# Summing gathered expert rows in 64x64 blocks of the TensorE array, two rows at a time, with one PSUM bank fewer for the context's mixer

## What is computed

```python
qry = (x @ w_query).reshape(n, 8, 2, 128)           # 8 heads
s = einsum('nhpd,hpkd->nhpk', qry, sub_keys)        # 128 keys on either side
# top 16 of each side, top 16 of their sums: 16 experts of 16384 per head and token
w = softmax(top_s)
a = gelu(einsum('nd,nhkd->nhk', xb, expert_u[ib]))  # 128 u rows per token
coef = w * a
x = x + g2 * einsum('nhk,nhkd->nd', coef, expert_v[ib])  # 128 v rows per token
```

## Time and profile before

| | |
|---|---|
| time, three runs | 4953.61, 4959.36, 4966.07 us; median 4959.36 |
| span of the profiled execution, first to last instruction | 4933.1 us |
| its own time beside the span | not listed apart; the median run is 26.3 us above this span |
| mean granted TensorE clock | 0.947 |
| busy share: PE, DVE, GpSimd, ACT | 80%, 62%, 57%, 24% |
| moved by DMA | 1585.40 MB, mean 321 GB/s |
| latents' V places, layer 0 | from 1105 to 2686 us |
| latents' V places, layer 1 | from 3468 to 4900 us |

### The profile page before, as it was taken

One profiled execution on the slowest core, in us unless ns is written; L12 is line 12 of the kernel. 1 busy time (PEld: TensorE's weight loads), 2 busy tenths in 40 slices (PEclk: granted clock), 3 DMA queues, 4 the chain that ended last, 5 costly groups with the idle time before them and its releaser, 6 DMA issues.

```text
span 4933.1 us, 40947 instructions
## 1 busy us (share of the span) xinstructions
PE 3932.0 (80%) x11544; PEld 1863.3 (38%) x11544; DVE 3078.9 (62%) x6951; ACT 1199.2 (24%) x2524; POOL 2831.9 (57%) x2642
## 2 busy tenths in 40 slices
PE   5798889889777777788776787999787777777776
PEld 3674444334333333344342454444332222222222
DVE  8637898775556556555655777852557566566653
ACT  2433333211223222232111343231112111111111
POOL 0001556317677677777766444630767777777775
PEclk8798889999999999999999898999999999999999
DMA  8653889758999999999988766962889999999997
GB/s 306 230 180 144 295 312 389 272 199 318 345 365 358 356 379 379 379 400 400 380 327 336 254 230 238 369 242 79 313 333 379 367 384 383 370 398 383 389 392 299
DMA packets 425891, 1585.40 MB, mean 321 GB/s; under 512 B 47680, under 2 KB 55360, under 8 KB 408640
## 3 DMA queue, kind: packets, MB, share of 16 engines
q0 software_dynamic: 376800, 1394.77, 74.8%
q1 hardware_dynamic: 44256, 183.81, 10.0%
q10 hardware_dynamic: 4608, 4.20, 0.3%
HBM read 1577.87 MB, written 4.72 MB: 321 GB/s over the span
## 4 chain that ended last, share of the span: by engine, by line
PE 20%; DMA 18%; issue 5%; POOL 3%; DVE 2%; ACT 1%; DVEq 1%; ACTq 0%; POOLq 0%
PE pair L744 19%; DMA vbuf_lat<-in_expert_v,idx_lat 17%; POOL ubuf_lat L709 2%; POOL vbuf_lat L716 1%; DVE acc L1747 0%; PE pair L880 0%; PE pair L885 0%; DMA ubuf_ctx<-in_expert_u,idx_ctx 0%; DVE ubuf_ctx L1698 0%; DMA ubuf_lat<-in_expert_u,idx_lat 0%; ACT L1128 0%; DVEq L1569 0%; DVE hist_lat L1566 0%; DVEq L1741 0%; ACT on_lat L1128 0%
## 5 line engine op out<-in xcount | busy, mean ns | idle before, releaser
L744 PE MATMUL pair<-vbuf_lat,diag 128*128 128x512 f32 x4096 | 2036.2, 629 | 706.6 <-DMA vbuf_lat<-in_expert_v,idx_lat 674.6
L744 PEld LDWEIGHTS pair<-vbuf_lat,diag 128*128 128x128 f32 x4096 | 731.8, 195 | 1946.4 <-DMA vbuf_lat<-in_expert_v,idx_lat 1042.3
L716 POOL DMA_INDIRECT vbuf_lat<-in_expert_v,idx_lat x1024 | 1133.9, 1107 | 464.8 <-issue 220.1
L1698 DVE CUSTOM_DVE_ANT_0 ubuf_lat<-hT,ubuf_lat 128x1024 f32<-128x1024 f32 x768 | 936.1, 1224 | 702.2 <-DMA ubuf_lat<-in_expert_u,idx_lat 698.1
L709 POOL DMA_INDIRECT ubuf_lat<-in_expert_u,idx_lat x1024 | 1089.9, 1064 | 376.8 <-issue 226.2
L744 PE MATMUL pair<-hT,slot 128*128 128x512 f32 (+1 forms) x2048 | 578.3, 442 | 24.4 <-DVE hT L1428 15.9
L1128 ACT ACTIVATE diag<-cst,coef 128x128 f32<-128x128 f32 x1024 | 326.6, 390 | 1004.4 <-DVE coef L1704 1000.4
L709 POOL DMA_INDIRECT ubuf_ctx<-in_expert_u,idx_ctx x256 | 292.3, 1142 | 482.7 <-DVE araw L1698 307.3
L1698 DVE CUSTOM_DVE_ANT_0 ubuf_lat<-xnat,ubuf_lat 128x1024 f32<-128x1024 f32 x256 | 312.0, 1224 | 250.4 <-DMA ubuf_lat<-in_expert_u,idx_lat 248.3
L744 PEld LDWEIGHTS pair<-hT,slot 128*128 128x128 f32 x2048 | 319.2, 196 | 275.4 <-issue 262.4
L1128 ACT ACT_TABLE_LOAD x318 | 408.0, 1283 | 31.9 <-DVE mT_lat L1592 15.2
(11 more groups left out here) (313 smaller groups left out, 3148.7 us busy)
## 6 DMA issues: line engine op xcount, KB each, us to landing
slot<-in_w_query SPq DMA_DIRECT2D x32, 1024.0 KB, 5.6
modw<-in_w_mod_turned POOLq DMA_DIRECT2D x28, 1024.0 KB, 5.7
slot<-in_w_qk SPq DMA_DIRECT2D x16, 1024.0 KB, 6.8
slot<-in_w_v SPq DMA_DIRECT2D x16, 1024.0 KB, 5.9
slot<-in_w_r SPq DMA_DIRECT2D x16, 1024.0 KB, 7.9
wraw<-in_w_zg SPq DMA_DIRECT2D x32, 512.0 KB, 6.5
wraw<-in_w_zf SPq DMA_DIRECT2D x32, 512.0 KB, 6.5
wraw<-in_w_gla_out SPq DMA_DIRECT2D x32, 512.0 KB, 6.5
```

The source lines that it names most:

```text
L716: pool.indirect_dma_start(peer[s].v[n % ring_v][:, :], None, v_rows, bass.IndirectOffsetOnAxis(ap=index[:, p // PICKS, p % PICKS:p % PICKS ...
L744: return pe.matmul(out, lhsT, rhs, start=first, stop=last)
L1698: v.tensor_tensor_reduce(rows_of, x, rows_of, 1.0, 0.0, ALU.mult, ALU.add, araw[n % 3][:, p % GS:p % GS + 1]).then_inc(s_dot, 1)
```

## The change

- The latents' V rows are added two places at a time. PE waits for both places' rows and then, for each half of the 1024 columns, issues four matmuls of 64x64 by 64x512: each place's diagonal is cut in its two 64x64 diagonal blocks, which stand in the four different quadrants of the array. The blocks of partitions 0 to 63 write to `pair[0]`, those of 64 to 127 to `pair[1]`; an odd place writes to the other half of the partitions. Both places are marked as added (`s_pv`) by matmuls of the second half of the columns.
- So the sums lie in four banks, in two parts each. ACT makes two copies of 128x1024 at a tile's end, and `turn_latents_out` adds the parts while it transposes: two matmuls by a 128x64 matrix `fold` for each 128 columns, in place of one transpose, now in `ps[7]`.
- `fold` is made by DVE at the start, from the identity; DVE waits for the constants' DMA (`s_const`) ahead of it.
- The context's mixer has `ps[4]` to `ps[6]`. Its products go round three banks; its two state steps share one pair of banks, so the second waits for DVE's update of the first.
- The latents' queries use `ps[6]`, `ps[7]`; the turned natural tiles use `pair[2]` for `pair[0]` (latents) and for `pair[3]` (context, layer 1), with waits that go with this. The first query no longer waits for the context's update; the first V group does.
- `iota` is stored in 32 columns and not 128.

```diff
-                    for j in range(GS):
-                        p = n * GS + j
-                        r = ring_no(l, s, p)
-                        pe.wait_ge(s_gv[s][r % V_RING[s]], gathered(V_RING[s], r))
+                    for j0 in range(0, GS, 2):
+                        for j in (j0, j0 + 1):
+                            r = ring_no(l, s, n * GS + j)
+                            pe.wait_ge(s_gv[s][r % V_RING[s]], gathered(V_RING[s], r))
                         for q in range(2):
-                            last = mm(pair[1][:, q * 512:(q + 1) * 512], diag[n % 2][:, j, :],
-                                      p1.v[r % V_RING[s]][:, q * 512:(q + 1) * 512], p % PICKS == 0, p % PICKS == PICKS - 1)
-                        last.then_inc(s_pv[s], 1)
+                            for j in (j0, j0 + 1):
+                                p = n * GS + j
+                                row = p1.v[ring_no(l, s, p) % V_RING[s]]
+                                for g in range(2):
+                                    own, to = slice(64 * g, 64 * g + 64), 64 * (g ^ j % 2)
+                                    last = mm(pair[g][to:to + 64, q * 512:(q + 1) * 512], diag[n % 2][own, j, own],
+                                              row[own, q * 512:(q + 1) * 512], p % PICKS < 2, p % PICKS >= PICKS - 2)
+                                if q == 1:
+                                    last.then_inc(s_pv[s], 1)
...
-            def turn_out(l, s, t, half, source):
+            def turn_latents_out(t, half):
+                for k in range(4 * half, 4 * half + 4):
+                    dst = turned(LAT, k % 4)
+                    for g in range(2):
+                        last = mm(dst[:, g * 64:(g + 1) * 64], out_nat[t][:, g, k * P:(k + 1) * P], fold[:, :], True, True)
+                last.then_inc(s_ot[LAT], 1)
...
                 def sums_copied(t):
                     act.wait_ge(s_pv[s], (tile_no(l, s, t) + 1) * PICKS)
-                    af(out_nat[t][:, :], pair[1][:, :], ACT.Copy).then_inc(s_on2, 1)
+                    for g in range(2):
+                        last = af(out_nat[t][:, g, :], pair[g][:, :], ACT.Copy)
+                    last.then_inc(s_on2, 1)
...
-                b.all = ps[4:8]
+                b.all = ps[4:7]
...
-            b.step = [(ps[6], ps[7]), (ps[4], ps[5])] if s == CTX else [(ps[2], ps[6]), (ps[3], ps[7])]
+            b.step = [(ps[6], ps[4]), (ps[6], ps[4])] if s == CTX else [(ps[2], ps[6]), (ps[3], ps[7])]
...
-                        if i >= 2:
-                            pe.wait_ge(s_st, step_no(l, s, h) + i - 1)
+                        if i >= (1 if s == CTX else 2):
+                            pe.wait_ge(s_st, step_no(l, s, h) + (i if s == CTX else i - 1))
...
-                        else:
-                            pe.wait_ge(s_xu[CTX], 2 * (l + 1))
+                        if h == PART + 1 and j == 0:
+                            pe.wait_ge(s_xnc, x0 + 1)
...
+            dve.wait_ge(s_const, 16)
+            tt(fold[:, :], ident[:, 0:64], ident[:, 64:128], ALU.add)
             dve.wait_ge(s_cols, 16)
```

More of the change, by code:

```diff
@@ L77 @@
 ZF0 = ZG0 + D
-C_ID, C_IOTA, C_ROT, C_COS, C_SIN = 0, 128, 256, 384, 896
-C_MF, C_MB, C_RESET, C_CDSD = 1408, 1536, 1664, 2176
-C_W = 2432
+C_ID, C_IOTA, C_ROT, C_COS, C_SIN = 0, 128, 160, 288, 800
+C_MF, C_MB, C_RESET, C_CDSD = 1312, 1440, 1568, 2080
+C_W = 2336
 SLOTS = 4
@@ L328, in build @@
     one = place("one", [P, 1])
+    fold = place("fold", [P, P // 2])
     columns = place("columns", [P, 24 + 80 * DEPTH])
@@ L445, in build @@
     assert q[0] <= area[CTX].end
-    out_nat = [place(f"out_nat{t}", [P, D], at=[area[CTX].end + t * PH * 2 * P * 4]) for t in range(NT[LAT])]
+    out_nat = [place(f"out_nat{t}", [P, 2, D], at=[area[CTX].end + t * PH * 2 * P * 4]) for t in range(NT[LAT])]
     peer[LAT].wts = place("wts_lat", [P, NT[LAT], PICKS], at=e)
@@ L460, in build @@
     rotT = cst[:, C_ROT:C_ROT + 128]
-    iota = cst[:, C_IOTA:C_IOTA + 128]
+    iota = cst[:, C_IOTA:C_IOTA + TOPK]
     cos, sin = cst[:, C_COS:C_COS + TS], cst[:, C_SIN:C_SIN + TS]
@@ L481, in mix_banks, with turned @@
                 b.all = ps[2:8]
-            b.U = ps[7][:, 0:n]
-            b.lr = ps[7][0:2 * LOWRANK, 0:n]
+            b.U = ps[6][:, DV:DV + n] if s == CTX else ps[7][:, 0:n]
+            b.lr = ps[6][0:2 * LOWRANK, 0:n] if s == CTX else ps[7][0:2 * LOWRANK, 0:n]
+            b.four = [ps[4][:, 0:n], ps[5][:, 0:n], ps[6][:, 0:n], ps[4][:, n:2 * n]] if s == CTX else [x[:, :] for x in ps[2:6]]
             b.ss = ps[6][:, 0:n]
-            b.step = [(ps[6], ps[7]), (ps[4], ps[5])] if s == CTX else [(ps[2], ps[6]), (ps[3], ps[7])]
+            b.step = [(ps[6], ps[4]), (ps[6], ps[4])] if s == CTX else [(ps[2], ps[6]), (ps[3], ps[7])]
             return b
         bank = [mix_banks(CTX), mix_banks(LAT)]
+        def turned(s, i):
+            return ps[0][:, i * P:(i + 1) * P] if s == CTX else ps[7][:, i * P:(i + 1) * P]
         def sem(name):
@@ L922, in mix @@
                             c0 = (t * 2 + q) * n
-                            last = mm(b.all[g][:, 0:n], a.ab[:, t, g, q, :], a.table[:, c0:c0 + n], t == 0 and q == 0, t == nt - 1 and q == 1)
+                            last = mm(b.four[g], a.ab[:, t, g, q, :], a.table[:, c0:c0 + n], t == 0 and q == 0, t == nt - 1 and q == 1)
                 last.then_inc(s_f2, 1)
@@ L971, in turn_x, with turn_context_out @@
                 last.then_inc(s_xn, 1)
-            def turn_out(l, s, t, half, source):
+            def turn_context_out(half):
                 for k in range(4 * half, 4 * half + 4):
-                    at = (k - 4 * half) * P
-                    last = pe.transpose(ps[0][:, at:at + P], source[:, k * P:(k + 1) * P], ident)
-                last.then_inc(s_ot[s], 1)
+                    last = pe.transpose(turned(CTX, k % 4), acc[:, k * P:(k + 1) * P], ident)
+                last.then_inc(s_ot[CTX], 1)
+            def turn_latents_out(t, half):
[4 more added lines that the diff above has]
+                last.then_inc(s_ot[LAT], 1)
             def context_queries(l, at):
@@ L1018, in context_sums @@
                     need(pe, s_xu[s], 2 * l + half if half else 0)
-                    turn_out(l, s, 0, half, acc)
+                    turn_context_out(half)
             def latent_queries(l):
@@ L1035, in natural @@
                 def natural(t):
-                    turn_x(l, s, t, pair[3 if t % 2 == 0 else 0])
+                    turn_x(l, s, t, pair[3 if t % 2 == 0 else 2])
                 x0 = l * (NT[0] + NT[1]) + NT[0]
@@ L1053, in latent_queries @@
                                 pe.wait_ge(s_h[s], (2 * l + 1) * KC + k + 1)
-                            last = mm(ps[j][:, :], w[:, k, j * P:(j + 1) * P], hT[:, k, COLS[s]], k == 0, k == KC - 1)
+                            last = mm(ps[6 + j][:, :], w[:, k, j * P:(j + 1) * P], hT[:, k, COLS[s]], k == 0, k == KC - 1)
                         last.then_inc(s_qm, 1)
@@ L1097, in latent_sums @@
                             need(pe, s_xu[s], 2 * tile_no(l, s, t - 1))
-                        turn_out(l, s, t - 1, half, out_nat[t - 1])
+                            pe.wait_ge(s_xnc, l * (NT[0] + NT[1]) + NT[0] + NT[1])
+                        turn_latents_out(t - 1, half)
                 for half in range(2):
@@ L1103, in latent_sums @@
                     pe.wait_ge(s_xu[s], 2 * tile_no(l, s, t) + half)
-                    turn_out(l, s, t, half, out_nat[t])
+                    turn_latents_out(t, half)
             def last_norm(s, at):
@@ L1247, in mix @@
                 for g in range(GROUPS):
-                    last = af(a.fourT[:, g, :], b.all[g][:, 0:n], ACT.Copy)
+                    last = af(a.fourT[:, g, :], b.four[g], ACT.Copy)
                 last.then_inc(s_f2c, 1)
@@ L1333, in latent_queries @@
                         act.wait_ge(s_qm, 2 * (n0 + h) + j + 1)
-                        af(p1.qry[h % 2][:, j, :], ps[j][:, :], ACT.Copy).then_inc(s_qc, 1)
+                        af(p1.qry[h % 2][:, j, :], ps[6 + j][:, :], ACT.Copy).then_inc(s_qc, 1)
                     if 1 <= h < LATE_HEADS:
@@ L1348, in latent_queries @@
                     yield natural_us(t) + 2.0
-                    natural(l, s, t, pair[3 if t % 2 == 0 else 0], in_place(s, t))
+                    natural(l, s, t, pair[3 if t % 2 == 0 else 2], in_place(s, t))
             def latent_sums(l):
@@ L1713, in update @@
                 for k in range(4 * half, 4 * half + 4):
-                    last = stt(xT[:, k, at], ps[0][:, (k % 4) * P:(k % 4 + 1) * P], modT[l][:, 40 + k, s:s + 1], xT[:, k, at],
+                    last = stt(xT[:, k, at], turned(s, k % 4), modT[l][:, 40 + k, s:s + 1], xT[:, k, at],
                                ALU.mult, ALU.add)
```

7 lines of the change are left out of this document (5 added, 2 removed).

## The result

The changed kernel takes 5520.34 us (median of four runs, 5515.23 to 5529.08), the kernel before 4956.48 in the four runs that it is compared with: a ratio of 1.1153, 95% interval 1.1126 to 1.1180. It is slower, as forecast, but by 564 us where the forecast had 241; the time lies above the range.

A forecast was written before the change was run, and what follows sets the result against it. In the long stretches it took V rows' DMA as the bound, PE waiting, with the V ring's loop closing under pairs. 4933 + 139 + 76 + 0 + 8 + 8 + 9 = 5173, plus 26: 5199, said 5200 us; range 4930 to 5330.

The forecast's parts named there:

- The pair's wait: V ring: a pair starts with its second row and releases both buffers at its end; 2.74 us per place, taken 2.80.
- the clock falls: Layer 1's long stretch: lower clock for two thirds, 3.03 us per place, +139 us with the pair's wait; chance 0.60.
- The start: Kernel start: DVE waits for the constants before everything else, so PE gets `hT` later; +8 us.
- The small costs: Start, context's mixer and tile ends: +8, +8 and +9 us, 25 together.
- The mixer's merging loop: Context's mixer with three banks, layer 0: loop from merge to merge of 7.3 us against 6.4; mixer +8 us in all.
- D falls as the DMA queue shortens, so I take 5.6: Pair's loop in layer 1: second V gather lands after 5.6 us at full clock, 5.4 at the lower; median before 6.5.
- at the full clock I leave the place at 3.04: Layer 0's long stretch: no loss at full clock, 3.40 per place at the lower, half the time each; +76 us.
- the query stretches: The two short latent stretches with queries (217 and 212 us): change 0, within 30 us either way.
- The 26 us that the sum adds: Final sum: the runs' median lies 26.3 us above the profiled span of 4933.1, carried over as time outside the span.
- the clock holds: Rival: clock stays near 0.97 despite gaps, the pair's wait still costs; about 5035 us; chance 0.15.
- faster: Rival: PE's halved work ends GpSimd's waits for PE, 112 us at most; about 4905 us; chance 0.17.
- no overlap: Rival: the four quadrants don't run side by side, a pair takes 7.9 us; near 6050 us; chance 0.03.

The follow-up runs named there:

- number 2: Changed kernel without its pairs: one place at a time, its two diagonal blocks in two quadrants; 4994.18 us, ratio 1.0062.
- number 3: Changed kernel with six V and four U buffers for the latents, in place of four and six; 5021.20 us, ratio 1.0114.
- 5: Changed kernel with the latents' gathers of two places in the order U, U, V, V; 5234.10 us, ratio 1.0556.
- number 1: Changed kernel plus sixteen zero-weight records (the zero blocks) after each pair in layer 1's long stretch; 5472.07 us, ratio 1.1023.
- Number 6: Kernel before, multiplying only the left 512 V columns except at a tile's first and last place; 4936.56 us, ratio 0.9959.
- 9: Changed kernel with five V and five U buffers, DVE's constants wait and fold moved behind the start's modulation rows; 5043.01 us, ratio 1.0175.
- 12: Changed kernel without pairs, with five V and five U buffers and the fold made later; 4927.01 us, ratio 0.9944.
- the fastest kernel: Kernel before with five V and five U buffers for the latents; 4897.98 us, ratio 0.9879.
- one that is 29 us slower than that: Kernel before with six V and four U buffers for the latents; 4926.52 us, ratio 0.9940.

## Why the prediction was wrong in its size

**Right:** what bounds the kernel, and the mechanism. Records in four quadrants run side by side (1.95 us for sixteen, taken 1.98; at 4148.4 the first four start within 0.05 us of each other, as forecast). GpSimd's real waits for PE before V gathers of layer 1's long stretch, those over the 0.3 us of every gather, went from 11 (16 us) to 142 (290 us), all 142 before even places, as forecast. The pair's wait closes the V ring's loop, the clock falls (0.64 in layer 1, forecast about 0.65) and the DMA share with it (0.88, forecast 0.9). The start cost 56.53 - 49.46 = 7.1 us in the trace and 9 alone, forecast 8. PE's first work on `hT` in the changed kernel:

```profile
56.53 3.82 PE L750 MATMUL pair<-hT,wlr_ctx 128*32 128x128 f32 x16 [17.36 <-DVE hT L1452]
```

The small costs together were 31, forecast 25. The mixer's merging loop, forecast at 7.3 us, has a period of 7.73 at first and then of 7.45:

```profile
219.74 1.95 PE L750 MATMUL pair<-oT_ctx,wraw 128*128 128x128 f32 x16
...
225.62 2.02 PE L750 MATMUL pair<-hT,wraw 128*128 128x128 f32 x16 [1.25 <-DVE mT_ctx L1616]
227.47 1.95 PE L750 MATMUL pair<-oT_ctx,wraw 128*128 128x128 f32 x16
...
234.92 1.95 PE L750 MATMUL pair<-oT_ctx,wraw 128*128 128x128 f32 x16
```

**The step that failed in layer 1** is the size of the loop's terms, and of these first "D falls as the DMA queue shortens, so I take 5.6", with 5.4 at the lower clock. Weighted as the prediction weights the two clocks, the loop comes to 12.1 us; measured are 13.5. D is the landing of a pair's second gather. It was 5.99 where I had 5.47 in the mean (+0.52): it fell from the 6.40 that V gathers took there in the mean before, but by 0.4 and not by 0.9. Then the burst was 3.41 where I had 3.18 (+0.23), the release 1.08 for 0.81 (+0.27), V to V 2.84 for 2.57 (+0.27), and the wait after landing 0.15 for nothing. That is 1.44, less 0.08 that I had added for unevenness: 1.36 us, 0.34 per place, 150 us, the gap between 139 and 287. All terms are off on one side. 2.57 and 0.81 were read from a steady place and from one release, and they are the usual case and not the mean: in the kernel before the median from V gather to V gather was 2.56 there and the mean 2.73. GpSimd's gather shows it too: 0.94 us is the median, the longest of V took 2.04, and its mean before was 1133.9 / 1024 = 1.11. Before, the loop had 1.0 us of slack by the prediction's own count; that this hid the long ones is argued and not shown.

**The step that failed in layer 0** is "at the full clock I leave the place at 3.04". There is no slack to leave it at: pairs that began at the full clock there had a loop of 14.5 us in the mean, 3.6 per place, against 12.2 for four places of 3.04. Those that began at the lower one had 14.2, forecast 13.6. In the mean over both the second gather's landing was 6.54, where I had 6.0, the wait before the burst 0.59 and the release 1.31. That term was to be +76 and was +234. Nor did the query stretches stay even, for which I took 0: they are 17 and 13 us longer, and without the pairs (number 2) 2 longer and 1 shorter.

**The clock had too large a part in my reasoning.** I put the pair's wait at the full clock at 36 us in layer 1 and the lower clock at 103 more. Numbers 3 and 5 show the clock low and all or half of the loss regained; number 1 shows the clock raised and 42 us regained. The changed kernel's own trace points the same way: in layer 1 the pairs that began at the full clock had a burst of 2.7 us and those that began at the lower one 3.6, and the loop took 13.5 us for both. The shorter burst met a longer release, 1.7 us against 0.9. Which pairs begin late and slow isn't chance, so this gives no price of the clock; with the zero blocks there was a difference, 12.9 us against 13.8. Landing, V to V and release make 5.99 + 2.84 + 1.08 = 9.9 of the loop's 13.5 us. The Trainium skill (TensorE: Matmul & The Clock Gate, section HAM oscillation — how this bites in real kernels) says that waits for DMA between short runs put the engine back to half rate. The trace agrees, at 0.64. It also books the slower share of the matmuls' time as time lost on the wall; number 1 does not bear that out here: of 193 us of PE's time at most 96 lay on the loop, and 42 came back.

**A wrong reading of little weight.** The 26 us that the sum adds don't lie outside the span. Every run took 1.8 us more than its span (5521.7 and 5519.9 here); the rest is the quick execution that was profiled. Against spans the forecast was +240 and the measurement +587, against medians +241 and +564.

**What the change could have brought** was the halved PE time. It did not arrive: a pair's burst of 3.41 us stands against 2 x 1.98 for two places before, 14% less and not 50%, since most pairs begin at 1.2 GHz. Number 6 shows the same with half of the work left out.

**Of the rivals**, "the clock holds" and "faster" fell by the clock and the loop, "no overlap" by the 1.95 us burst. (The cases' chances add up to 0.78 for slower and 0.17 for faster, where the last line has 0.77 and 0.18; nothing hangs on it.)

**Open** is why the pairs still cost 114 us at five buffers, 52 in layer 0's and 61 in layer 1's long stretch by the traces of numbers 9 and 12. By its terms the loop there, 10.4 us, is shorter than the 10.9 that the transfers of four places need, and no run separates its unevenness from the rest. With three pairs' worth of buffers (number 3) layer 1 loses nothing. What the clock is worth in number 1 is known only as between 42 and 96 us, since the zero blocks cost something themselves.

## What to carry to other kernels

Work in batches of two on a ring of four halves the ring: before merging waits, write the loop (gather to gather, landing, wait, burst, release) and compare it with what the ring's places take. Take the terms from means over the stretch, not from a steady place, once the slack is smaller than their spread, and let the landing time be that of the gather that closes the loop. When an engine waits for data at every step, giving it less work can lower its clock instead of its time; move a buffer from the ring that has slack to the one that hasn't first, which here gave 1.2%.

## What the runs showed of the hardware that I had not expected

- Half the matmuls took the same time: two records of the whole array in 2.07 us at a clock of 0.58, four in 1.98 at 0.99.
- V gathers that start 1.38 us apart and not 2.84 took only 0.22 us more to land in the mean of all, and the second of a pair, which the loop waits for, 0.05 more, while the DMA share went from 0.88 to 0.94.
- A pair's two gathers don't land alike: 5.45 us for the first and 5.99 for the second in layer 1, though both are the same transfer.
- The time that GpSimd waits for PE before V gathers says little about what it costs: 205 us before, 205 with half of the matmuls, 133 in the fastest kernel, 20 in one that is 29 us slower than that.
